# Encoder layer with a 32-expert mixture: bias matmuls moved into the activation wait, and the stream transposed between groups of the output projection

## The reference, cut to what matters

```python
h = h + o @ w_o                                # o: both attentions, each RMS-normalised, 1024 wide
hn = rmsnorm(h, g_xattn)
q = (hn @ w_mq).reshape(b, s, 4, 256)          # queries of the cross attention
...
logits = rmsnorm(h, g_moe) @ w_router + b_router   # 32 experts, the best 4 for each token
gu = xb @ w_gate_up[e] + b_gate_up[e]          # xb: the tokens of expert e
gate, up = jnp.split(gu, 2, axis=-1)
gate = jnp.minimum(gate, 7.0)
up = jnp.clip(up, -7.0, 7.0)
hmid = (up + 1.0) * (gate * jax.nn.sigmoid(1.702 * gate))
out = hmid @ w_down[e] + b_down[e]
```

## Time and profile before

| | us |
|---|---|
| median of 3 runs | 1214.39 |
| lowest and highest run | 1212.01, 1216.23 |
| span of the profiled execution | 1212.5 |
| that execution's own time | not given beside its span |
| TensorE's matmuls busy | 1162.4 (96% of the span) |
| VectorE, ScalarE busy | 301.7 (25%), 214.8 (18%) |
| first matmul of item 0, of item 32 | 291.79, 1174.37 |

### The profile page before, as it was taken

How to read it: one execution, slowest core, us unless ns; L and a number is a source line. 1 busy time by engine, 2 the same in 40 slices (tenths; PEclk the granted TensorE clock), 3 DMA queues, 4 the chain that set the end, 5 groups by cost and what they waited for, 6 DMA issues and landing times.

```text
span 1212.5 us, 13954 instructions
## 1 busy us (share of the span) xinstructions
PE 1162.4 (96%) x5355; PEld 477.2 (39%) x5355; DVE 301.7 (25%) x681; ACT 214.8 (18%) x404; POOL 6.6 (1%) x13
## 2 busy tenths in 40 slices
PE   9999999999999999999999999999999999999996
PEld 4476555854333333333333333333333333333332
DVE  3456543246221111111211111111111221111112
ACT  2110551221111111111111121111111111121112
POOL 0000010000000000000000000000000000000000
PEclk9999999999999999999999999999999999999999
DMA  9800378337999999999999999999999999999992
GB/s 361 354 1 1 126 274 328 139 139 295 430 426 429 426 431 431 427 436 432 430 430 431 429 427 437 431 432 416 409 431 425 436 432 432 422 428 426 429 425 83
DMA packets 29858, 440.27 MB, mean 363 GB/s; under 512 B 4592, under 2 KB 4848, under 8 KB 11152
## 3 DMA queue, kind: packets, MB, share of 16 engines
q1 hardware_dynamic: 28944, 439.32, 85.8%
q10 hardware_dynamic: 864, 0.19, 0.1%
HBM read 438.45 MB, written 1.05 MB: 362 GB/s over the span
## 4 chain that ended last, share of the span: by engine, by line
PE 85%; DMA 10%; ACT 2%; DVE 1%; issue 0%; POOLq 0%; ACTq 0%
PE quad L1481 32%; PE quad L1502 17%; DMA ring<-in_w_gate_up 10%; PE y_banks L1457 5%; PE quad L1441 4%; PE y_banks L1334 2%; PE y_banks L1118 2%; PE quad L1118 2%; PE quad L1449 2%; ACT work L613 2%; PE y_banks L1140 1%; PE quad L1467 1%; PE y_banks L1210 1%; PE y_banks L1281 1%; PE quad L1289 1%; PE quad L1390 1%
## 5 line engine op out<-in xcount | busy, mean ns | idle before, releaser
L1481 PE MATMUL quad<-ring,work 128*64 128x512 f32 x2112 | 463.1, 596 | 7.6 <-DMA ring<-in_w_gate_up 7.6
L1481 PEld LDWEIGHTS quad<-ring,work 128*64 128x64 f32 x2112 | 149.2, 138 | 303.0 <-issue 285.7
L1502 PE MATMUL quad<-ring,work 128*64 128x512 f32 x1056 | 233.9, 595 | 22.7 <-ACT work L613 22.7
L1502 PEld LDWEIGHTS quad<-ring,work 128*64 128x64 f32 x1056 | 72.9, 137 | 162.4 <-issue 131.9
L609 ACT ACTIVATE work<-work 128x512 f32<-128x512 f32 x33 | 20.8, 629 | 452.3 <-DVE work L1059 452.3
L1059 DVE TENSOR_SCALAR work<-quad 128x512 f32<-128x512 f32 x33 | 22.8, 691 | 306.2 <-PE quad L1481 306.2
L976 DVE CAST work<-cst 96x64 bf16 (+1 forms) x34 | 6.5, 191 | 287.9 <-PE quad L1481 287.9
L1457 PE MATMUL y_banks<-work 64*128 64x512 f32 x272 | 67.6, 615 | 0.7 <-ACT work L619 0.7
L1441 PE MATMUL quad<-h,work 128*64 128x512 f32 x272 | 64.1, 593 | 0.0
L617 ACT ACTIVATE work<-quad 128x512 f32<-128x512 f32 x33 | 19.7, 597 | 237.2 <-PE quad L1502 237.2
L609 ACT ACT_TABLE_LOAD x33 | 42.3, 1283 | 1.1 <-issue 0.5
(11 more groups left out here) (270 smaller groups left out, 824.9 us busy)
## 6 DMA issues: line engine op xcount, KB each, us to landing
ring<-in_w_gate_up SPq DMA_DIRECT2D x37, 4096.0 KB, 30.3
ring<-in_w_gate_up SPq DMA_DIRECT2D x54, 2048.0 KB, 21.7
ring<-in_w_down SPq DMA_DIRECT2D x18, 4096.0 KB, 29.0
ring<-in_w_down SPq DMA_DIRECT2D x28, 2048.0 KB, 20.3
ring<-in_w_mkv SPq DMA_DIRECT2D x8, 1024.0 KB, 23.9
ring<-in_w_in SPq DMA_DIRECT2D x7, 976.0 KB, 17.3
ring<-in_w_o SPq DMA_DIRECT2D x1, 4096.0 KB, 13.0
ring<-in_w_mq SPq DMA_DIRECT2D x1, 4096.0 KB, 22.8
```

What stands on the lines that cost most here:

```text
L1481: ins = mm(bank[n // 2][lo:lo + BLK, :], xgT[:, k % 4 * P + k // 4 * BLK:k % 4 * P + k // 4 * BLK + BLK], up_rows(j, k)[:, n * 512:(n + 1) ...
L1502: ins = mm(bank[3][n * BLK:(n + 1) * BLK, :], lhs, down_rows(j, f)[:, n * 512:(n + 1) * 512], start=(f == 0), stop=(f == KC - 1))
```

## The change

Three edits. In the experts' loop `biases` no longer opens an item: `biases(w + 1)` is issued in item `w` between the transposes of the hidden values and the wait for their copy, and `biases(0)` ahead of the first item, before the wait for the gates' copy. The wait for the gathered columns stays at the item's start. In the mixer the transposes of tile 0 go between groups 5 and 6 of the output projection, those of the first half of tile 1 into the middle of group 7, and those of its second half between query matmuls. The query matmuls begin with the first four input chunks of groups 2 and 0. VectorE's gains move accordingly.

```diff
@@ VectorE
+            def mixed_gained(t, b):
+                dve.wait_ge(S["hT_mm"], 2 * t + b + 1)
+                with_gain(hT_s[:, 4 * b:4 * b + 4, t * P:(t + 1) * P], spl(bank[2 * t + b][:, :], 4),
+                          G_X + 4 * b, 4, P).then_inc(S["hTs_ready"], 1)
+
             for j in range(8):
                 t, g, n = j // 4, j // 2 % 2, j % 2
+                if j == 6:
+                    mixed_gained(0, 0)
+                    mixed_gained(0, 1)
+                if j == 7:
+                    mixed_gained(1, 0)
                 dve.wait_ge(S["wo_mm"], j + 1)
...
-            gained(hT_s, S["hT_mm"], S["hTs_ready"], G_X, (0, 1, 2, 3))
+            mixed_gained(1, 1)
@@ TensorE
-            def mixed_out(j):
+            def mixed_out(j, ks=range(4)):
...
+            def mixed_columns(t, b):
+
+                pe.wait_ge(S["h_ready"], 4 * t + 3 + b)
+                for j in range(4):
+                    c = 4 * b + j
+                    ins = pe.transpose(bank[2 * t + b][:, j * P:(j + 1) * P], h[:, t, c * P:(c + 1) * P], ident)
+                ins.then_inc(S["hT_mm"], 1)
+
+            def mem_queries(c, ks):
+                for k in ks:
+                    ins = mm(bank[4 + c // 2][:, c % 2 * SEQ:(c % 2 + 1) * SEQ], wmq[:, k, c * P:(c + 1) * P], hT_s[:, k, :],
+                             start=(k == 0), stop=(k == KC - 1))
+                if c % 2 and ks[-1] == KC - 1:
+                    ins.then_inc(S["qm_mm"], 1)
...
                 if j == 7:
                     pe.wait_ge(S["ocol_read"], 1)
-                mixed_out(j)
-
-            transposes(h, S["h_ready"], 4, S["hT_mm"], (0, 1, 2, 3))
+                    mixed_out(j, range(0, 2))
+                    mixed_columns(1, 0)
+                    mixed_out(j, range(2, 4))
+                else:
+                    mixed_out(j)
+                if j == 5:
+                    mixed_columns(0, 0)
+                    mixed_columns(0, 1)
+
+            pe.wait_ge(S["hTs_ready"], 3)
+            pe.wait_ge(S["ld_wmq"], 16)
+            mem_queries(2, range(0, 4))
+            mixed_columns(1, 1)
+            mem_queries(0, range(0, 4))
             pe.wait_ge(S["hTs_ready"], 4)
-            pe.wait_ge(S["ld_wmq"], 16)
-            for c in range(KC):
...
+            mem_queries(0, range(4, KC))
+            mem_queries(1, range(KC))
+            mem_queries(2, range(4, KC))
+            for c in range(3, KC):
+                mem_queries(c, range(KC))
...
             def biases(w):
-                pe.wait_ge(S["xg_ready"], w + 1)
+
                 pe.wait_ge(S["bsel_ready"], w + 1)
...
             def item(w, j):
-                biases(w)
+                pe.wait_ge(S["xg_ready"], w + 1)
...
                 ins.then_inc(S["hid_mm"], 1)
+                biases(w + 1)
                 pe.wait_ge(S["hid_ready"], w + 1)
                 pe.wait_ge(S["xg_ready"], w + 2)
...
             ins.then_inc(S["gtT_mm"], 1)
+            biases(0)
 
             pe.wait_ge(S["gtT_ready"], 1)
```

More of the change, by code:

```diff
@@ L1284, in late_values @@
                     ins.then_inc(S["v_mm"], 1)
-            def mixed_out(j):
+            def mixed_out(j, ks=range(4)):
                 t, g, n = j // 4, j // 2 % 2, j % 2
-                for k in range(4):
+                for k in ks:
                     ins = mm(bank[WO_BANKS[j]][:, :], oT[:, 4 * g + k, t * P:(t + 1) * P],
                              wo[:, 4 * g + k, n * 512:(n + 1) * 512], start=(k == 0), stop=(k == 3))
-                ins.then_inc(S["wo_mm"], 1)
+                if ks[-1] == 3:
+                    ins.then_inc(S["wo_mm"], 1)
+            def mixed_columns(t, b):
[5 more added lines that the diff above has]
+            def mem_queries(c, ks):
+                for k in ks:
+                    ins = mm(bank[4 + c // 2][:, c % 2 * SEQ:(c % 2 + 1) * SEQ], wmq[:, k, c * P:(c + 1) * P], hT_s[:, k, :],
+                             start=(k == 0), stop=(k == KC - 1))
+                if c % 2 and ks[-1] == KC - 1:
+                    ins.then_inc(S["qm_mm"], 1)
             pe.wait_ge(S["q96_ready"], 4)
@@ L1326, in _ @@
                     pe.wait_ge(S["ocol_read"], 1)
-                mixed_out(j)
-            transposes(h, S["h_ready"], 4, S["hT_mm"], (0, 1, 2, 3))
-            pe.wait_ge(S["hTs_ready"], 4)
-            pe.wait_ge(S["ld_wmq"], 16)
-            for c in range(KC):
[L1333 to L1337, removed]
+                    mixed_out(j, range(0, 2))
[11 more added lines that the diff above has]
+            mem_queries(0, range(0, 4))
+            pe.wait_ge(S["hTs_ready"], 4)
+            mem_queries(0, range(4, KC))
[3 more added lines that the diff above has]
+                mem_queries(c, range(KC))
             def mem_scores(u):
```

## The result

The changed kernel takes 1205.2 us, median of 4 runs (1204.05 to 1205.57), against 1214.39: a ratio of 0.9922, 95% interval 0.9908 to 0.9936, or 9.2 us. The forecast was 1206.3. In this kernel an execution takes its span plus 1.8 us (1204.05 beside 1202.3), so the profiled execution of before, with its span of 1212.5, was one of about 1214.3, near the median, and that of after is its kernel's fastest run. The traces lie 10.2 us apart, the medians 9.2. Measured once more later, beside fresh runs of before, the medians lay 7.6 us apart (1204.95 against 1212.59), so the size is known to a microsecond or so and no better.

The account below looks back on a forecast made before the run. TensorE was taken to bind up to item 0, transfers until 823.7 us, then TensorE again. The terms 1.63 + 0.43 + 5.98 = 8.04 us came off 1214.39, giving 1206.3 us, range 1203.2 to 1212.4.

Parts of the forecast that it names:

- Three stretches with different limits: TensorE and partners limit up to item 0, transfers from there to 823.7 us, TensorE alone over the last 13 item starts.
- Part 1: Mixer transposes and query matmuls: 3.39 us becomes 1.76, at best 1.63 us gained; four margins of 0.7 to 0.9 us.
- Part 2: First bias block, ahead of item 0, moves into the wait for the gathered columns: 0.43 us gained.
- Part 3: Each item's bias block hides in the activation wait: 0.46 us an item, 5.98 us over 13 items.
- paid in both: Slow start behind the wait at 823.73 us, 1.7 us, assumed to occur in the old and the new kernel.
- 0 taken: Four slow residual matmul instructions ahead of item 0, 3.46 us against 1.8: no gain counted, 1.3 us either way.
- The lead at the end: Last item's fourth chunk lands 7.3 us before it is read; after 5.98 us of gain, 1.3 us left.
- 9.4 us: Without the new kernel's slow start behind 823.73 us, the lead caps that stretch's gain at 7.3 us: time 1205.0.
- The stream of transfers: From item 0 to 823.7 us, a queued transfer lands by the stream's start plus the bytes, 29.3 us an expert.
- Rival A: Transfers bind behind 823.7 us as well, leaving only the prologue's 2.06 us: 1212.3 us; chance 0.14.
- Rival B: The turn between items does not close up; at worst all 0.46 us stays, 1212.3 us; chance 0.15.
- Rival C: The bias block does not fit the activation wait, costing 0.96 us net an item: 1224.8 us; chance 0.04.

Follow-up runs that it names:

- wait_late: Changed kernel with the bias block kept at the item's start for experts 0 to 18: 1206.21 us.
- less_scatter: Without each item's scatter half for the second token tile (its output left out): 1201.68 us on the changed kernel, 1203.01 us on the kernel before.
- query_only: Kernel before with the output projection and query edits alone, without the bias edit: 1211.49 us, ratio 0.9976.
- bias_only: Kernel before with the bias edit alone, output projection and queries as before: 1207.56 us, ratio 0.9940.
- changed_again: The changed kernel itself, measured once more beside later variants: 1204.95 us, ratio 0.9927.
- refill_warm: Changed kernel with the edits of keep_warm and split_refill together: 1206.98 us.
- split_refill: Changed kernel with the first chunk loaded during the items fetched in two halves, the first issued earlier: 1205.72 us.
- keep_warm: Changed kernel with 4 unneeded matmul instructions ahead of the third weight chunk of each item of experts 12 to 18: 1205.49 us.
- double_bias: Changed kernel with the bias block issued twice in the activation wait: 1207.26 us.

## Why the prediction was right, point by point

- **Three stretches with different limits.** Shown: the table above for the middle one, `wait_late` for what an early item's saving is worth, the waits of the two `less_scatter` kernels for the end.
- **Part 1, 1.63 us.** The trace has 1.66 (223.79 - 222.13), `query_only` 1.75, so 1.63 was not quite the upper bound it was called; the query matmuls themselves got some 0.1 us shorter. All four margins held, with no wait in the timeline.
- **Part 2, 0.43 us.** From VectorE's gain to the first matmul it was 291.79 - 290.42 = 1.37 us and is 288.93 - 287.99 = 0.94: 0.43.
- **Part 3, 5.98 us.** The mechanism held, the size was off by 0.7. The turn shrank by 0.45, but the first chunk behind it now takes 0.05 us longer, the restart that the bias block used to take on itself; the item went from 27.09 to 26.68 or 26.69, 0.405 us. 13 of these are 5.3 us.
- **The clock.** Here the forecast of the gain came out too low, by its choice of "paid in both" and "0 taken". In the profile of after neither slow stretch is there, which makes 3.2 us between the two traces. The medians hold less of it: 9.2 less the 7.4 of the three terms as measured leaves 1.8 us; that these are the clock's is argued from the traces, since only one execution of a kernel has one. The forecast of 8.0 us lies close to 9.2 in part by luck: 0.7 too much in part 3 stands against 1.8 that was not counted. Of the other traces with a wait at that place, five have the slow start (`bias_only`, `wait_late`, `less_scatter`, `changed_again`, `refill_warm`) and six have not; the slow residual matmuls were in the trace of before alone.
- **The lead at the end.** Forecast 1.3 us left, measured 1.4, and that is luck too. TensorE comes to the chunk 10.2 us earlier, not 8.0, and the chunk lands 4.3 us earlier, not 2.1 (2.9 by item 0's start; the source of the other 1.4 is not shown). The "9.4 us" case, in which the lead caps what the clock gives, did not come in this trace: no transfer is waited for in the last item.
- **The stream of transfers.** "Its start plus the bytes" is too simple: `split_refill` brought the start forward by 1.2 us, and the landing did not move, since a later gap, set by item 0's pace, took it back.
- **Rival A** was not met by this change but stands right behind it: `less_scatter` gets 3.5 us for 12 of removed work. **Rival B** was worth its 0.05 us an item. **Rival C** did not come: 1.29 us unchanged, and even a second block costs 0.08.

## What to carry to other kernels

When a weight stream and the matmuls are near each other in speed, follow one transfer from issue to landing: if it stood in the queue for several times its own length, what is saved ahead of it is only worth what it moves the stream's start. Count the savings from the last transfer that the chain waits for, and measure the lead at the end, since it caps them. And a producer's wait is a good place for work that needs nothing of it, if the next use of the same engine leaves room in it: here 0.85 us of wait took the block of 0.46 us, and the down matmuls started as early as before.

## What had not been expected

**A slow start without idle time.** In `keep_warm` the granted clock fell while TensorE was busy:

```profile
1081.11 3.69 PE L1576 MATMUL y_banks<-work 32*128 32x512 f32 x8
1084.73 10.50 PE L1520 MATMUL quad<-ring,work 128*64 128x512 f32 x40
```

```profile
1080.00:1084.70 4.70, 4.70 (x14) 1.00 1.04 436
1084.70:1088.10 3.40, 3.40 (x11) 0.61 1.01 429
```

The columns of the second fence are the stretch, its length, TensorE busy (instructions), granted clock, DMA share and GB/s. A mean of 0.61 is mostly the lower of the two levels, 1.2 GHz, and it costs 1.7 us at item 29. What ran just before it, without a gap, were eight matmul instructions of the down bias, which use 32 of the 128 rows. Five of the traces have it (`double_bias`, both `less_scatter`, `keep_warm`, `split_refill`), the others not, with the same matmuls. That the few rows are the cause was only argued. The Trainium skill, TensorE: Matmul & The Clock Gate, "HAM oscillation — how this bites in real kernels", puts the throttle down to gaps in which TensorE stands idle; at this place no trace shows one.

**Where the spread of the runs comes from.** Of the 38 runs of the kernel before beside the experiments, the seven with a mean clock of 0.996 or more took 1211.7 to 1212.4 us, the 24 with 0.993 or 0.994 took 1213.9 to 1216.0, and the seven with 0.995 lie on both sides (1212.1 to 1214.8). The two slow stretches of its trace that cost time are worth 3.2 us together, so they can make up most of the 4 us of spread; no run but the profiled one shows where its clock fell. The clock alone is no measure, though: `keep_warm` has 0.996 to 0.998 and is no faster, and slow starts ahead of a wait for transfers are free, since the wait shrinks by what they cost.

**The transposes at the end had been useful filler.** Moving them forward without the half groups made the stage 0.4 us longer (224.2 us against 223.8; from the fifth group of the output projection to the first score matmul 45.2 against 44.9), because they had covered part of the wait for the last residual.
